# Gate matmuls begun one half tile later and packed six to a body, the gelu of a tile applied one half tile later

## The chip, the cores and the metric

The kernel runs on one core of a Trainium2 chip. The metric is the time of one launch on the device in microseconds (us), as the median of several runs. The engines named below are TensorE (PE in the profile; PEld is its weight load), VectorE (DVE), ScalarE (ACT), GpSimd (POOL) and SyncE (SP). A name with a q behind it (ACTq, DVEq, SPq) is the queue of that engine, that is the instructions that it issues or skips over without computing.

## The reference

Two layers, each a mixer (four kinds of attention over 256 tokens of width 2048) and a feed-forward block of 16384 experts, with a layer norm behind each. The change is in the feed-forward block, `peer_ffn`:

```python
q = x @ wq                                  # 8 heads, two halves of 128 each
s = einsum('blhpc,hpnc->blhpn', q, sub_keys)
s1, i1 = top_k(s[..., 0, :], 16)            # 16 of 128 first keys
s2, i2 = top_k(s[..., 1, :], 16)            # 16 of 128 second keys
cand = s1[..., :, None] + s2[..., None, :]  # 256 sums
top_s, pos = top_k(cand, 16); eidx = cidx[pos]
g = softmax(top_s)                          # gate of each chosen expert
h = einsum('td,tkd->tk', x, u[eidx])        # only the chosen experts
out = einsum('tk,tkd->td', g * gelu(h), v[eidx])
```

The kernel does not gather experts. It computes h for all 16384 experts, applies gelu to all, builds a dense table of gates (zero where an expert is not chosen) and multiplies.

## The kernel before, in words

**The stream.** The rows of u come as 128 tiles of 128x2048 (1 MB each) from the chip's memory, in order, through four buffers `raw0` to `raw3`. A tile is worked in two halves of 128x1024. For each half ACT rounds it to a high part (`split_hi`, L625, the copy at L634), DVE computes the low part as the difference (`split_lo`, L913, the subtraction at L917), and PE multiplies both with the tokens (`hidden`, L532: eight pairs of matmuls, L371 with 512 columns and L372 with 256). There are four buffers for the high parts and four for the low parts, so `split_hi` of half n+4 waits until `hidden` of half n is done, and ACT and DVE issue it in step n. Eight halves (four tiles) are called a body. A layer's u stream is 32 bodies, in four quarters of eight.

**A tile's result.** After the odd half of a tile, ACT copies one half of the result out of the bank (`take_cross`, L749, L754), DVE adds the other half (`add_cross`, L1221, L1223), ACT applies gelu in place (`gelu`, L756, L759) and issues a DMA that stores it in memory (L761). Tiles use banks 0 and 1 in turn, and `hidden` of a tile's even half waits for `add_cross` of the tile two before.

**The quarters.** For each of the two blocks of 128 tokens (b = 0, 1) there is a route quarter and a build quarter. In a route quarter DVE does, beside the splits, the top-k selection of one head per body (`route_body`, L1235). In a build quarter 32 gate steps are made, each for 4 tokens: POOL writes one-hot rows of the first keys (`first_keys`, L858: a copy at L861 and four operations at L864), DVE those of the second keys with their weights (`second_keys`, L1314: four operations at L1319), PE multiplies the two (`gate_step`, L542 ff., L551), and ACT copies the product into the table `gates` (`place_gates`, L765, L771). Each of these has two buffers: keys for step s wait until gate step s-2 is done.

**The first body of a build quarter** closes the softmax. DVE subtracts the largest score (`gate_weights`, L1301 and L1302) and then takes step 0. ACT applies Exp behind its step 1 (L797), which needs another function table than gelu, so a table load comes before it and another before the next gelu. DVE computes the sums and scales behind its step 2 (`gate_sums`, L1308 to L1310, semaphore `routed`). PE waits for `routed` behind `hidden` of half 3, turns the selected numbers with three transposes (L569), and ACT stores them (`sel_t`, L800) behind its own step 3. Then come gate steps behind halves 4 to 7. The other seven bodies have a gate step behind each odd half, the very last body behind halves 1, 3, 5 and 6.

**Order.** The order of each engine's work is written by hand. In step j of a body, ACT's `half_body` (L774) does `take_cross` if j is odd, `split_hi` of half j+4, and if j is odd `gelu` of the tile whose `take_cross` it has just done. DVE's `build_split` (L1338) does `add_cross` if j is odd and `split_lo` of half j+4. SP issues the loads of tiles in order, waits for the 32 gate steps of b = 0 before the loads of body 17, and writes the table of gates to memory between the loads of bodies 17 to 20. `place_gates` for b = 1 waits for these writes.

**Behind the stream** the same kind of loop runs over v (L590 to L592). It begins when the last `add_cross` is done. In its last step of the u stream DVE makes the first products of gelu and gate, and ACT their high part, `a_high` (L812), one step earlier in its order.

Of the kernel before, what the change touches and what calls it, by code (L numbers as in the profile page):

```python
# [15 lines left out]
P = 128  # L16
DEPTH, D, L = 2, 2048, 256
NB = L // P
# [6 lines left out]
NRAW, NSPLIT = 4, 4  # L25
BODY = 2 * NRAW
# [62 lines left out]
def build(nc, x_in, w_in, w_out, wq, keys, u_t, v_t, ln, sinks, lamp, subg, layer_consts,  # L89
# [6 lines left out]
    with ExitStack() as ctx:  # L96
# [47 lines left out]
        qk_t, at = region(0, 32, L)  # L144
        vals, at = region(at, NB, V_END)
# [9 lines left out]
        ln_gb, at = region(0, 2, D)  # L155
# [22 lines left out]
        STEPS = P // TG  # L178
        quarter = N_U // BODY // 4
        assert quarter == PH and STEPS == quarter * NRAW  # L180
        LAST_STEPS = (1, 3, 5, 6)
        PIECES = 16
        ROWS = NKEY // PIECES
        oh1 = [scr[:, i * 512:(i + 1) * 512].rearrange("p (t n) -> p t n", n=NKEY) for i in range(2)]
# [65 lines left out]
        with nc.Fori(0, DEPTH) as layer:  # L250
# [7 lines left out]
            with nc.Block() as block:  # L258
# [90 lines left out]
                def _(pe):  # L349
# [207 lines left out]
                    for b in range(NB):  # L557
                        if b == 0:
                            for j in range(BODY):
                                hidden(0, j, first=j < 4)  # L560
                        with pe.Fori(2 * b * quarter + (b == 0), (2 * b + 1) * quarter) as i:
                            for j in range(BODY):
                                hidden(i, j)
                        for j in range(BODY):
                            hidden((2 * b + 1) * quarter, j)
                            if j == 3:
                                pe.wait_ge(routed, b + 1)
                                for k in range(3):
                                    last = pe.transpose(bank[2][:, k * P:(k + 1) * P], sel[:, k, b, :], ident[:])  # L569
                                last.then_inc(sel_turned, 1)  # L570
                            if j >= 4:
                                gate_step(b * STEPS + j - 4, j % 2, first=(b == 0 and j < 6))
                        with pe.Fori(1, quarter - b) as i:
                            for j in range(BODY):
                                hidden(i + (2 * b + 1) * quarter, j)
                                if j % 2:
                                    gate_step(i * 4 + (b * STEPS + j // 2), j // 2 % 2)
                    for j in range(BODY):
                        hidden(4 * quarter - 1, j)
                        if j in LAST_STEPS:  # L580
                            gate_step(2 * STEPS - 4 + j // 2, j // 2 % 2)


                    def products(b, j, slot, start=False, stop=False):
# [39 lines left out]
                def _(act):  # L624
# [149 lines left out]
                    def half_body(i, j, first=False, last=False):  # L774

                        if j % 2:
                            take_cross(i, j // 2, i * 2 + j // 2 // 2, first=first and j < 4)
                        ahead = j + NSPLIT
                        if not last or ahead < BODY:
                            split_hi(AT_U, i + ahead // BODY, ahead % BODY)  # L780
                        else:
                            split_hi(AT_V, 0, ahead % BODY)
                        if j % 2:
                            gelu(i, j // 2)

                    for b in range(NB):
                        if b == 0:
                            for j in range(BODY):
                                half_body(0, j, first=True)
                        with act.Fori(2 * b * quarter + (b == 0), (2 * b + 1) * quarter) as i:  # L790
                            for j in range(BODY):
                                half_body(i, j)
                        for j in range(BODY):
                            half_body((2 * b + 1) * quarter, j)
                            if j == 1:
                                act.wait_ge(gate_arg, b + 1)
                                act.activation(sel[:, 2, b, :], sel[:, 2, b, :], ACT.Exp).then_inc(gate_exp, 1)  # L797
                            if j == 3:
                                act.wait_ge(sel_turned, b + 1)
                                act.activation(sel_t[:, :, b * P:(b + 1) * P], bank[2][:, 0:3 * P].rearrange("p (s t) -> p s t", s=3),  # L800
                                               ACT.Copy).then_inc(sel_stored, 1)
                            if j >= 4:
                                place_gates(b * STEPS + j - 4, (j - 4) * TG, j % 2, b)
                        with act.Fori(1, quarter - (b == 1)) as i:
                            for j in range(BODY):
                                half_body(i + (2 * b + 1) * quarter, j)
                                if j % 2:
                                    place_gates(i * 4 + (b * STEPS + j // 2), i * (4 * TG) + j // 2 * TG, j // 2 % 2, b)

                    def a_high(i, m):  # L810
                        act.wait_ge(prod_done, i * NRAW + (m + 1))
# [1 line left out]

                    for j in range(BODY):
                        half_body(4 * quarter - 1, j, last=True)
                        if j in LAST_STEPS:
                            place_gates(2 * STEPS - 4 + j // 2, P - 4 * TG + j // 2 * TG, j // 2 % 2, 1)
                        if j == BODY - 2:

                            a_high(0, 0)  # L820
# [80 lines left out]
                def _(dve):  # L901
# [432 lines left out]
                    def a_low(i, m):  # L1334
                        dve.wait_ge(ah_done, i * NRAW + (m + 1))
                        dve.tensor_tensor(al[m % 2], prod[m % 2], ah[m % 2].bitcast(F32), ALU.subtract).then_inc(al_done, 1)
# [7 lines left out]
                        else:  # L1344
                            split_lo(AT_U, i + (2 * b + 1) * quarter + ahead // BODY, ahead % BODY)

                    def build_body(i, b, last=False):

                        for j in range(BODY):
                            if b == NB - 1 and last and j == BODY - 1:  # L1350
                                dve.wait_ge(gate_evac, NB * STEPS)
                                product(0, 0, first=True)
                                product(0, 1, first=True)
                                a_low(0, 0)
                            build_split(i, b, j, last=last)
                            if j % 2 and not (last and j == BODY - 1):
                                second_keys(i * NRAW + (b * STEPS + j // 2 + 1), (j // 2 + 1) % 2)

                    def first_build_body(b):

                        gate_weights(b)
                        for j in range(BODY):
                            build_split(0, b, j)
                            if j == 2:
                                gate_sums(b)
                            if j == 3:
                                dve.wait_ge(sel_stored, b + 1)
                            if j >= 3:
                                second_keys(b * STEPS + j - 3, (j - 3) % 2, first=(b == 0 and j < 5))

                    for b in range(NB):
                        with dve.Fori(0, PH) as h:
                            route_body(h + 2 * b * quarter, b, h)
                        first_build_body(b)
                        with dve.Fori(1, quarter - 1) as i:
                            build_body(i, b)
                        build_body(quarter - 1, b, last=True)

                    def second_body(i, last=False):
                        for j in range(BODY):  # L1380
# [104 lines left out]
```

## Time and profile before

| | |
|---|---|
| median of 3 runs | 4180.57 us (4180.12 to 4183.09) |
| the profiled execution's own time | 4183.27 us |
| its span, first to last instruction | 4181.4 us |
| PE busy | 4052.1 us (97%), weight loads 3416.7 us (82%) |
| DVE busy | 2695.9 us (64%) |
| ACT busy | 1976.2 us (47%) |
| POOL busy | 515.8 us (12%) |
| mean granted TensorE clock | 0.959 of 2.4 GHz |

Busy time is an average over the whole span. What a stage is bound by is read from single stretches: from the time line of one engine, where an idle time stands in square brackets at the end of a row with what ended it, and from tables over stretches of time.

### The profile page before, as it was taken

To read this page: it belongs to the slowest core of one execution; us is meant where nothing else is said; L and a number is where in the kernel's file an instruction comes from. 1 tells how busy PE (TensorE), PEld (TensorE's weight loads), DVE (VectorE), ACT (ScalarE), POOL (GpSimd) and SP (SyncE) were. 2 spreads that over 40 slices of the span, in tenths; PEclk is the share of its full clock that TensorE was granted. 3 is DMA by queue.
4 is the path that set the end of the run, shared out by engine and by line. 5 is a ranking of instruction groups with operands and counts; after the bars stand their busy time and mean duration, and the time that the engine had idled before them with its cause. 6 is when DMAs were issued, how large, how long until landed. Compare 5 with 4: busy or idle time off the path is not lost. (4 is left out here: it accounts for less than half of the span.)

```text
span 4181.4 us, 64897 instructions
## 1 busy us (share of the span) xinstructions
PE 4052.1 (97%) x20356; PEld 3416.7 (82%) x20356; DVE 2695.9 (64%) x5308; ACT 1976.2 (47%) x2824; POOL 515.8 (12%) x728
## 2 busy tenths in 40 slices
PE   8999899999999999999899998999999999999997
PEld 7877788888888888888678777888888888888886
DVE  5656658767866555555656655686678665555556
ACT  4444344555455444444344443445554554444443
POOL 0100000351045000000001000003510550000000
PEclk9967999999999999999999779999999999999999
DMA  6512455557655666666545124555586556666664
GB/s 221 191 61 82 180 179 203 191 182 246 230 181 189 221 231 249 226 228 231 175 171 190 51 101 177 180 206 185 181 259 224 178 192 222 227 250 231 230 226 177
DMA packets 243054, 810.75 MB, mean 194 GB/s; under 512 B 24321, under 2 KB 157441, under 8 KB 157441
## 3 DMA queue, kind: packets, MB, share of 16 engines
q1 hardware_dynamic: 206080, 775.78, 52.9%
q10 hardware_dynamic: 36864, 33.57, 2.3%
q8 instruction: 62, 1.02, 0.1%
q14 instruction: 48, 0.39, 0.0%
HBM read 756.82 MB, written 52.43 MB: 194 GB/s over the span
## 5 line engine op out<-in xcount | busy, mean ns | idle before, releaser
L917 DVE TENSOR_TENSOR lo<-raw,hi 128x1024 fp32r<-128x1024 f32 x1312 | 1640.7, 1252 | 1194.4 <-ACT hi L634 1165.5
L634 ACT ACTIVATE hi<-raw 128x1024 fp32r<-128x1024 f32 x1312 | 1388.4, 1059 | 1366.9 <-PE bank L592 759.1
L371 PE MATMUL bank<-xhl,hi 128*128 128x512 f32 x4608 | 1641.4, 400 | 5.4 <-DVE xhl L923 2.8
L372 PE MATMUL bank<-xhl,lo 128*128 128x256 f32 x4608 | 1291.8, 280 | 0.0
L371 PEld LDWEIGHTS bank<-xhl,hi 128*128 128x128 f32 x4608 | 869.2, 189 | 212.0 <-DVE gelu_out L1223 3.9
L372 PEld LDWEIGHTS bank<-xhl,lo 128*128 128x128 f32 x4608 | 873.4, 190 | 0.0
L590 PE MATMUL bank<-hi,xhl 128*128 128x512 f32 x2048 | 797.1, 389 | 2.2 <-DVE gelu_out L1223 1.9
L592 PE MATMUL bank<-hi,xhl 128*128 128x512 f32 x2048 | 796.7, 389 | 0.0
L591 PE MATMUL bank<-lo,xhl 128*128 128x512 f32 x2048 | 796.7, 389 | 0.0
L590 PEld LDWEIGHTS bank<-hi,xhl 128*128 128x128 f32 x2048 | 384.4, 188 | 83.3 <-DVE gelu_out L1223 2.5
L592 PEld LDWEIGHTS bank<-hi,xhl 128*128 128x128 f32 x2048 | 384.4, 188 | 80.0
L591 PEld LDWEIGHTS bank<-lo,xhl 128*128 128x128 f32 x2048 | 384.4, 188 | 79.7
L864 POOL TENSOR_SCALAR scr<-iota_k,small 128x128 f32<-128x128 f32 x512 | 404.8, 807 | 12.2
L383 PE MATMUL bank<-hi,xhl 128*128 128x512 f32 (+1 forms) x896 | 352.6, 393 | 9.7 <-DVE lo L917 6.0
L385 PE MATMUL bank<-hi,xhl 128*128 128x512 f32 (+1 forms) x896 | 348.9, 389 | 0.0
L384 PE MATMUL bank<-lo,xhl 128*128 128x512 f32 (+1 forms) x896 | 348.6, 389 | 0.0
L874 POOL TENSOR_TENSOR x<-x,arena 128x512 f32<-128x512 f32 x8 | 13.4, 1679 | 1939.9 <-ACT x L731 1939.9
L754 ACT ACTIVATE gelu_out<-bank 128x256 f32<-128x256 f32 x256 | 97.0, 379 | 262.3 <-PE bank L372 262.3
L759 ACT ACTIVATE gelu_out<-gelu_out 128x256 f32<-128x256 f32 x256 | 105.9, 414 | 238.1 <-DVE gelu_out L1223 238.0
L383 PEld LDWEIGHTS bank<-hi,xhl 128*128 128x128 f32 x896 | 168.9, 189 | 43.5 <-issue 6.4
L385 PEld LDWEIGHTS bank<-hi,xhl 128*128 128x128 f32 x896 | 168.8, 188 | 34.8
L384 PEld LDWEIGHTS bank<-lo,xhl 128*128 128x128 f32 x896 | 169.2, 189 | 33.0
(131 smaller groups left out, 2692.7 us busy)
## 6 DMA issues: line engine op xcount, KB each, us to landing
raw<-u_t SPq DMA_DIRECT2D x256, 1024.0 KB, 4.8
raw<-v_t SPq DMA_DIRECT2D x256, 1024.0 KB, 4.8
raw<-w_in SPq DMA_DIRECT2D x84, 1024.0 KB, 4.8
raw<-w_out SPq DMA_DIRECT2D x32, 1024.0 KB, 4.8
raw<-wq SPq DMA_DIRECT2D x32, 1024.0 KB, 4.8
gelu_scratch<-gelu_out ACTq DMA_DIRECT2D x256, 128.0 KB, 1.7
scr<-gelu_scratch SPq DMA_DIRECT2D x256, 128.0 KB, 4.6
gates_scratch<-arena SPq DMA_DIRECT2D x32, 512.0 KB, 9.5
```

Of the source, the lines that this page charges most:

```text
L371: pe.matmul(acc[:], wh, xhl[:, c, :, :].rearrange("p a t -> p (a t)"), start=(c == 0), stop=False)
L372: return pe.matmul(acc[:, L:2 * L], wl, xh[:, c, :], start=False, stop=(c == DC - 1))
L383: pe.matmul(banks[b][:, 0:width], st_h, mh, start=(c == first_c), stop=False)
L384: pe.matmul(banks[b][:, 0:width], st_h, ml, start=False, stop=False)
L385: last = pe.matmul(banks[b][:, 0:width], st_l, mh, start=False, stop=(c == last_c))
L590: pe.matmul(y, a_h, vh, start=start, stop=False)
L591: pe.matmul(y, a_h, vl, start=False, stop=False)
L592: last = pe.matmul(y, a_l, vh, start=False, stop=stop)
L634: act.activation(hi[j % NSPLIT][:], half, ACT.Copy).then_inc(hi_done, 1)
L759: act.activation(gelu_out[m % 2][:], gelu_out[m % 2][:], ACT.Gelu).then_inc(gelu_done, 1)
L864: last = pool.tensor_scalar(oh1[p][:, t, :], iota_k[:], key_cols[p][:, t:t + 1], None, ALU.is_equal)
L917: dve.tensor_tensor(lo[j % NSPLIT][:], half, hi[j % NSPLIT][:].bitcast(F32), ALU.subtract).then_inc(lo_done, 1)
```

## The change

`hidden`, `gate_step`, `place_gates`, `first_keys`, `second_keys` and `gelu` stay as they are. Their places in the order change. In the first build body PE's wait for `routed` and the transposes stand behind half 4 instead of half 3, gate steps follow halves 6 and 7 only, ACT's copy of `sel_t` stands behind its step 4, and DVE's wait for it behind its step 4. The next five bodies have six gate steps each, behind halves 0, 1, 3, 4, 6 and 7. The last two bodies of each build quarter have none. `gelu` of a tile is applied in ACT's next even step, behind `split_hi`. The last tile's gelu stays in the last step.

```diff
-        LAST_STEPS = (1, 3, 5, 6)
+        STEP_OF = {0: 0, 1: 1, 3: 2, 4: 3, 6: 4, 7: 5}
+        PER_BODY = len(STEP_OF)
+        BUILD = (STEPS - 2) // PER_BODY
...
                         for j in range(BODY):
                             hidden((2 * b + 1) * quarter, j)
-                            if j == 3:
+                            if j == 4:
                                 pe.wait_ge(routed, b + 1)
...
-                            if j >= 4:
-                                gate_step(b * STEPS + j - 4, j % 2, first=(b == 0 and j < 6))
-                        with pe.Fori(1, quarter - b) as i:
+                            if j >= 6:
+                                gate_step(b * STEPS + j - 6, j % 2, first=(b == 0))
+                        with pe.Fori(1, 1 + BUILD) as i:
                             for j in range(BODY):
                                 hidden(i + (2 * b + 1) * quarter, j)
-                                if j % 2:
-                                    gate_step(i * 4 + (b * STEPS + j // 2), j // 2 % 2)
...
+                                if j in STEP_OF:
+                                    gate_step(i * PER_BODY + (b * STEPS + 2 - PER_BODY + STEP_OF[j]), STEP_OF[j] % 2)
+                        with pe.Fori(1 + BUILD, quarter) as i:
+                            for j in range(BODY):
+                                hidden(i + (2 * b + 1) * quarter, j)
...
-                        if j % 2:
+                        if j % 2 == 0 and not (first and j == 0):
+                            gelu(i, j // 2 - 1)
+                        if last and j == BODY - 1:
                             gelu(i, j // 2)
...
-                            if j == 3:
+                            if j == 4:
                                 act.wait_ge(sel_turned, b + 1)
...
+                    STEP_AHEAD = {1: -2, 2: -1, 4: 0, 5: 1, 6: 2, 7: 3}
...
+                            if j in steps:
+                                second_keys(i * PER_BODY + (b * STEPS + STEP_AHEAD[j]), STEP_AHEAD[j] % 2)
...
-                            if j == 3:
+                            if j == 4:
                                 dve.wait_ge(sel_stored, b + 1)
-                            if j >= 3:
-                                second_keys(b * STEPS + j - 3, (j - 3) % 2, first=(b == 0 and j < 5))
+                            if j >= 4:
+                                second_keys(b * STEPS + j - 4, j % 2, first=(b == 0 and j < 6))
```

## Rows read from the trace of the kernel before

**Rows 1.** PEld's time line, first build bodies (start us, us, engine, line, operation, [idle])
```profile
776.33 0.19 PEld L372 LDWEIGHTS bank<-xhl,lo 128*128 128x128 f32 x1
780.66 0.31 PEld L569 LDWEIGHTS bank<-ident,sel 128*128 128x128 f32 x3 [4.14 <-DVE sel L1310]
780.94 0.19 PEld L371 LDWEIGHTS bank<-xhl,hi 128*128 128x128 f32 x1
785.38 0.97 PEld L551 LDWEIGHTS bank<-scr 128*128 128x128 f32 x8
...
1171.03 0.19 PEld L372 LDWEIGHTS bank<-xhl,lo 128*128 128x128 f32 x1
1180.82 1.13 PEld L551 LDWEIGHTS bank<-scr 128*128 128x128 f32 x8
...
2857.59 0.19 PEld L372 LDWEIGHTS bank<-xhl,lo 128*128 128x128 f32 x1
2867.80 0.98 PEld L551 LDWEIGHTS bank<-scr 128*128 128x128 f32 x8
...
3252.94 0.19 PEld L372 LDWEIGHTS bank<-xhl,lo 128*128 128x128 f32 x1
3263.36 0.98 PEld L551 LDWEIGHTS bank<-scr 128*128 128x128 f32 x8
```

**Rows 2.** Waits of PEld over the span (us in total, times, longest)
```profile
PEld bank L569 <- DVE sel L1310: 17.6, 4, 4.8
```

**Rows 3.** PE in a stretch (us, busy, instructions, granted clock, DMA share, GB/s)
```profile
2865.00:2867.00 2.00, 2.00 (x8) 0.50 0.80 242
```

**Rows 4.** ACT's time line, first build body, layer 1, b = 0
```profile
2857.12 0.42 ACT L759 ACTIVATE gelu_out<-gelu_out 128x256 f32<-128x256 f32 x1 [1.53 <-DVE gelu_out L1223]
2857.95 1.28 ACT L797 ACT_TABLE_LOAD   x1 [0.41 <-ACT gelu_out L759]
2859.24 0.31 ACT L797 ACTIVATE sel<-sel 128x128 f32<-128x128 f32 x1
2859.46 1.04 ACT L634 ACTIVATE hi<-raw 128x1024 fp32r<-128x1024 f32 x1
```

**Rows 5.** DVE's time line, same body
```profile
2855.32 0.29 DVE L1302 TENSOR_TENSOR sel<-sel,small 128x128 f32<-128x128 f32 x1
2860.53 1.23 DVE L917 TENSOR_TENSOR lo<-raw,hi 128x1024 fp32r<-128x1024 f32 x1 [2.32 <-ACT hi L634]
2862.22 0.29 DVE L1310 TENSOR_TENSOR sel<-sel,small 128x128 f32<-128x128 f32 x1
```

**Rows 6.** Time lines of ACT and DVE, steps 5 and 6 of a route body
```profile
2754.66 0.42 ACT L759 ACTIVATE gelu_out<-gelu_out 128x256 f32<-128x256 f32 x1 [2.35 <-DVE gelu_out L1223]
2756.79 1.22 DVE L917 TENSOR_TENSOR lo<-raw,hi 128x1024 fp32r<-128x1024 f32 x1 [0.53 <-ACT hi L634]
```

**Rows 7.** PEld's time line, the same wait in two following route bodies
```profile
2789.36 0.19 PEld L371 LDWEIGHTS bank<-xhl,hi 128*128 128x128 f32 x1 [0.52 <-DVE gelu_out L1223]
...
2812.35 0.19 PEld L371 LDWEIGHTS bank<-xhl,hi 128*128 128x128 f32 x1 [0.60 <-DVE gelu_out L1223]
```

**Rows 8.** First matmuls L371 alone in route stretches, layers 0 and 1
```profile
670.00:770.00 100.00, 100.00 (x285) 1.00 0.59 209
...
2670.00:2770.00 100.00, 100.00 (x290) 1.00 0.56 194
```

**Rows 9.** PEld's time line, start of layer 1's route quarters, and a gate step
```profile
2666.49 0.19 PEld L371 LDWEIGHTS bank<-xhl,hi 128*128 128x128 f32 x1 [0.88 <-ACT scr L745]
...
3060.91 0.97 PEld L551 LDWEIGHTS bank<-scr 128*128 128x128 f32 x8
3061.81 0.19 PEld L371 LDWEIGHTS bank<-xhl,hi 128*128 128x128 f32 x1
```

**Rows 10.** PEld's time line, start of the v stream, layer 1
```profile
3458.66 0.19 PEld L590 LDWEIGHTS bank<-hi,xhl 128*128 128x128 f32 x1 [1.25 <-DVE gelu_out L1223]
```

**Rows 11.** All of line L864 (count, duration ns min/median/max, first and last start)
```profile
L864 POOL TENSOR_SCALAR scr<-iota_k,small x512: 594/602/1692, 783.0 to 3447.6; 128x128 f32<-128x128 f32 x171
```

More of the change, by code:

```diff
@@ L180, in build @@
         assert quarter == PH and STEPS == quarter * NRAW
-        LAST_STEPS = (1, 3, 5, 6)
+        STEP_OF = {0: 0, 1: 1, 3: 2, 4: 3, 6: 4, 7: 5}
+        PER_BODY = len(STEP_OF)
+        BUILD = (STEPS - 2) // PER_BODY
+        assert 2 + BUILD * PER_BODY == STEPS and BUILD < quarter - 1
         PIECES = 16
@@ L570, in _ @@
                                 last.then_inc(sel_turned, 1)
-                            if j >= 4:
-                                gate_step(b * STEPS + j - 4, j % 2, first=(b == 0 and j < 6))
-                        with pe.Fori(1, quarter - b) as i:
+                            if j >= 6:
+                                gate_step(b * STEPS + j - 6, j % 2, first=(b == 0))
+                        with pe.Fori(1, 1 + BUILD) as i:
                             for j in range(BODY):
                                 hidden(i + (2 * b + 1) * quarter, j)
-                                if j % 2:
-                                    gate_step(i * 4 + (b * STEPS + j // 2), j // 2 % 2)
[L578 to L581, printed above, removed]
+                                if j in STEP_OF:
[3 more added lines that the diff above has]
+                                hidden(i + (2 * b + 1) * quarter, j)
                     def products(b, j, slot, start=False, stop=False):
@@ L801, in _ @@
                                                ACT.Copy).then_inc(sel_stored, 1)
-                            if j >= 4:
-                                place_gates(b * STEPS + j - 4, (j - 4) * TG, j % 2, b)
-                        with act.Fori(1, quarter - (b == 1)) as i:
+                            if j >= 6:
+                                place_gates(b * STEPS + j - 6, (j - 6) * TG, j % 2, b)
+                        with act.Fori(1, 1 + BUILD) as i:
                             for j in range(BODY):
                                 half_body(i + (2 * b + 1) * quarter, j)
-                                if j % 2:
-                                    place_gates(i * 4 + (b * STEPS + j // 2), i * (4 * TG) + j // 2 * TG, j // 2 % 2, b)
+                                if j in STEP_OF:
+                                    at = 2 - PER_BODY + STEP_OF[j]
+                                    place_gates(i * PER_BODY + (b * STEPS + at), i * (PER_BODY * TG) + at * TG, STEP_OF[j] % 2, b)
+                        with act.Fori(1 + BUILD, quarter - (b == 1)) as i:
+                            for j in range(BODY):
+                                half_body(i + (2 * b + 1) * quarter, j)
                     def a_high(i, m):
@@ L815, in _ @@
                         half_body(4 * quarter - 1, j, last=True)
-                        if j in LAST_STEPS:
-                            place_gates(2 * STEPS - 4 + j // 2, P - 4 * TG + j // 2 * TG, j // 2 % 2, 1)
                         if j == BODY - 2:
@@ L1345, in build_split, with build_body @@
                             split_lo(AT_U, i + (2 * b + 1) * quarter + ahead // BODY, ahead % BODY)
-                    def build_body(i, b, last=False):
+                    STEP_AHEAD = {1: -2, 2: -1, 4: 0, 5: 1, 6: 2, 7: 3}
+                    def build_body(i, b, steps=STEP_AHEAD):
                         for j in range(BODY):
[L1350 to L1357, printed above, removed]
+                            build_split(i, b, j)
+                            if j in steps:
+                                second_keys(i * PER_BODY + (b * STEPS + STEP_AHEAD[j]), STEP_AHEAD[j] % 2)
                     def first_build_body(b):
@@ L1365, in first_build_body, with last_build_body @@
                                 gate_sums(b)
-                            if j == 3:
+                            if j == 4:
                                 dve.wait_ge(sel_stored, b + 1)
-                            if j >= 3:
-                                second_keys(b * STEPS + j - 3, (j - 3) % 2, first=(b == 0 and j < 5))
+                            if j >= 4:
+                                second_keys(b * STEPS + j - 4, j % 2, first=(b == 0 and j < 6))
+                    def last_build_body():
+                        for j in range(BODY):
+                            if j == BODY - 1:
+                                dve.wait_ge(gate_evac, NB * STEPS)
+                                product(0, 0, first=True)
+                                product(0, 1, first=True)
+                                a_low(0, 0)
+                            build_split(quarter - 1, NB - 1, j, last=True)
                     for b in range(NB):
@@ L1374, in _ @@
                         first_build_body(b)
-                        with dve.Fori(1, quarter - 1) as i:
+                        with dve.Fori(1, BUILD) as i:
                             build_body(i, b)
-                        build_body(quarter - 1, b, last=True)
+                        build_body(BUILD, b, steps=(1, 2, 4, 5))
+                        with dve.Fori(1 + BUILD, quarter - (b == 1)) as i:
+                            build_body(i, b, steps=())
+                    last_build_body()
                     def second_body(i, last=False):
```

## The prediction

> **What bounds the kernel now.** I read the page's busy shares first, then the chain of waits, then PE's weight loads in order of time through the u stream, since a matmul's own end is modelled and the start of its weight load is not. PE issues without a break nearly everywhere, so the question is where it does not. The reader is to see three places.
>
> First, in each of the four first build bodies PE stops behind half 3 until DVE's L1310, 17.6 us over four waits [rows 2]. Behind the stop the clock is at the lower of its two levels, 1.2 GHz, where it had been at 2.4 GHz without a break before it [rows 3], so half 4 is slow as well.
>
> Second, in layer 1's route quarters PE waits once or twice a body for DVE's `add_cross`; the same wait returns after 2812.35 - 2789.36 = 22.99 us [rows 7].
>
> Third, before the v stream it waits 1.25 us [rows 10].
>
> Two units follow. In layer 1 a pair of matmuls takes 100/290 = 0.345 us, in layer 0 100/285 = 0.351 us [rows 8]. Some records may be missing, and from pair to pair the loads step by 0.3467 and 0.3533 us. A half of eight pairs is thus 2.77 or 2.83 us, a body 22.2 or 22.6 us, at the same full clock and from the same code. A gate step takes 3061.81 - 3060.91 = 0.90 us [rows 9].
>
> **Step 1, the wait for `routed`.** From the last load of half 3 to gate step 0 the four bodies take 9.05, 9.79, 10.21 and 10.42 us [rows 1], 39.47 us in all. Without wait and slow clock it would be the last pair's rest of 0.23, the transposes 780.94 - 780.66 = 0.28 and a half of 2.77, so 3.28 us each. The excess is 39.47 - 13.12 = 26.3 us: 17.6 us of waits [rows 2], the rest the slow clock.
>
> Does all of it go? Count from the end of half 3, E = 2857.8 in layer 1, b = 0 (last load plus 0.23). Now: gelu at 2857.12, the DMA issue behind it, table load at 2857.95, Exp at 2859.24, the high part at 2859.46 [rows 4], DVE's low part at 2860.53 and L1310 done at 2862.51, E + 4.7 [rows 5]. DVE had its operand for Exp ready at 2855.61, E - 2.2, and Exp stood in ACT's queue behind a gelu that waited for DVE.
>
> New: no gelu stands between `split_hi` of step 1 and Exp. The copy and the high part of step 1 need half 1, done at E - 5.5, and end by E - 4.1. Table load and Exp run from E - 2.2 to E - 0.6, the high part to E + 0.4, the low part to E + 1.7, `gate_sums` takes from the end of the low part, 2861.76, to 2862.51, another 0.75 [rows 5]: `routed` at E + 2.4. PE asks for it at E + 2.8, behind half 4. In layer 0 the pace is slower and DVE further ahead, which gives more room. So the wait goes and with it the fall of the clock: -26.3 us. The margin is 0.4 us, and step 2 adds to it. Bounds: if only the half tile of 2.77 us helped, -11.1 us; with nothing left over, -26.3.
>
> The Trainium skill says in ScalarE: Activation LUTs, What ACT_TABLE_LOAD costs, that a switch of table takes about 2.66 us, 1.28 of load and 1.38 of drain. By that, `routed` could come as late as E + 3.8 and PE would still wait 1.0 us four times, leaving 4 us. This trace shows the load (1.28 us) with Exp 0.01 us behind it and only 0.41 us before it, DMA issue included [rows 4].
>
> **Step 2, gelu one half tile later.** In a route body ACT's gelu of step 5 starts at 2754.66 when DVE has added, its DMA and `split_hi` of step 6 queue behind it, and DVE idles 0.53 us for that high part [rows 6]. DVE is otherwise without a gap and is what holds PE there; its body is 22.99 us [rows 7] against PE's 22.2. With gelu behind `split_hi`, that high part is made when half 6 is done, some 4 us before DVE wants it. DVE's body becomes 22.99 - 0.53 = 22.46 us.
>
> DVE starts a route quarter with a lead. It lost 0.8 us a body against the fast pace, and the first stalls of PE come near 2777, after 4.8 bodies: the lead is 3.8 us. Eight bodies of 22.46 cost 8 x 0.27 = 2.2 us of it, so PE never waits. Layer 1's two quarters take from 2666.49 and from 3061.81 to 2857.82 and 3253.17, 191.3 us each [rows 1, 9]; 68 halves of 2.77 are 188.6. Gain 2.7 each, -5.5 us. In layer 0 DVE loses only 0.4 us a body against the slow pace and PE never waits for it: nothing to gain. The cover is the two tiles between a gelu and the reuse of its buffer; the store of 128 KB lands in 1.7 us by the page, far inside it. Bounds: 0 and -5.5.
>
> At the last step the high part of the first product now stands before `take_cross` with no gate step on PE to cover it: low part done 2.3 us behind half 6, product 0.5, high part 0.4, so `take_cross` begins at 3.3 us instead of the 2.8 at which half 7 ends. PE's wait of 1.25 us [rows 10] grows by about 0.6 us, in two layers +1.2 us (bounds 0 and +2).
>
> **Step 3, the packing.** PE's count of halves and gate steps stays the same. Behind a gate come either one half or two, so gates start 3.67 or 6.4 us apart. ACT does at most a high part, a gelu with its issue and one placing (1.06 + 0.9 + 1.1 = 3.1 us) in 3.67. POOL takes 4 x 0.602 [rows 11] + 0.3 = 2.7 us a step alone. DVE's key operations for a gate stand two halves before it. I find no wait in the bodies of six: 0.
>
> In the first body gate steps 0 to 3 come 3.67 us apart, as before, when they came 3.9 apart because POOL or DVE was just late. The copy of `sel_t` now ends 2.6 us behind half 4 (high part and gelu go first), the first keys of POOL 2.8 us later, and PE arrives at 6.0. I take the small waits as they are: 0, bounds +2 and -2.4.
>
> The two bodies without gates run at a body's 22.2 or 22.6 us. Behind a gate the pace was the fast one in two tiles of three before; a slow pace costs 0.43 a body, eight bodies: +0.9, bounds 0 and +3.4. SP's wait for the 32 gates ends earlier, its writes move ahead by a few halves, with loads that no one waits for: 0.
>
> **Sum.** -26.3 - 5.5 + 1.2 + 0.9 = -29.7 us. The profiled execution took 4183.3 and would take 4153.6; it was 2.7 us above the median of the runs, 4180.57, from which the same difference gives 4151 us.
>
> **Rivals.** (a) The pace of PE falls the other way. It is picked anew behind each stop and I can't derive it. If layer 1's route quarters run at 2.83 us a half, 2 x 68 x 0.053 = 7.2 us are lost and with all bodies without gates slow another 2.5: 4161 us. For it: layer 0 is slow in both quarters. Against: layer 1 is not. If layer 0 turns fast instead it is 4144; I count that with the forecast.
>
> (b) The wait is only shortened, since the margin of 0.4 us is thin and a chain of ten instructions sets it. PE then waits one to two us, which does not lower the clock (the 1.25 us before the v stream didn't, its loads go on at 0.23 us): 4 x 1.5 = 6 us more, with half the clock's gain at risk: 4157 to 4166, say 4161.
>
> (c) Slower than before: POOL. The longest L864 is 1692 ns against 602 [rows 11], one low part of DVE (1.2 us) longer. Gates behind halves 6, 7, 0 and 1 are the tight place: POOL may begin the third's keys when the first is done, and both third and fourth must be ready 10.1 us later, so it decides when a key step averages over 5.07 us. With one low part caught it is 3.8, with two 4.9, with three 6.0. At 6.0 PE waits 2 x 0.93 = 1.9 us in each of the 20 packed bodies, 37 us in all, which outweighs the gain: 4188. Against it: a body has eight low parts for six steps, and before the change a step caught one. The Trainium skill, SBUF — State Buffer, on its shared port pair, makes this an exclusive lock between these two engines, held for a whole instruction; by the maximum above the trace agrees.
>
> (d) The stop does not go but moves: PE passes `routed` and stops before gate step 0, where keys begin only after `sel_t`. The cover is 6.0 us against 5.4 needed. To eat the whole gain it must be over 5 us and drop the clock again: 4178.
>
> **How the numbers follow.** Forecast 0.68, (a) 0.14, (b) 0.09, (c) 0.05, (d) 0.04. A measurement of this kernel tells 0.2% (8.4 us) from no change. Forecast, (a) and (b) are faster by more than that: 0.91, of which I take 0.01 off for their tails; same 0.05, slower 0.05. Low end: 29.7 + 7.2 (layer 0 fast) + 2.4 (small waits gone) gives 4141. High end: (a) and (b) at 4161 with the 3 us by which runs differ, 4164.
>
> **What would show it.** Right: in all four first build bodies the load of L569 follows the last L372 by about 0.23 us with no idle time, the granted clock stays 1.00 through them, and last load of half 4 to gate step 0 is 6.1 us. In the route quarters DVE's 0.53 us at the sixth step and PE's waits for L1223 are gone. L864 may show more long operations but PE none waiting at L551 in packed bodies. The idle time before the first L590 is near 1.9 us. Wrong: an idle time over 1 us before L569 or L551, a clock of 0.5 anywhere in the u stream, or waits of PE that repeat with a body's period.

## The result, and the profile after the change

The kernel after the change takes 4158.15 us (median of 4 runs, 4155.05 to 4160.42) against 4180.92 for the kernel before (4 runs, 4180.12 to 4183.09). The ratio is 0.9944, its 95% interval 0.9930 to 0.9959: 22.8 us less, where 29.7 were forecast. In a later batch the same kernel took 4156.31 us (5 runs, 4151.98 to 4158.62), a ratio of 0.9940, 0.9927 to 0.9954. The profiled execution took 4160.42 us, with a span of 4158.6 and a mean granted clock of 0.962 (before 0.959).

The page's first part, busy us with shares and instruction counts, and its fourth, the chain that ended last:

```profile
PE 4043.6 (97%) x20356; PEld 3411.6 (82%) x20356; DVE 2689.6 (65%) x5308; ACT 1969.0 (47%) x2824; POOL 516.6 (12%) x728
...
PE 48%; DVE 1%; ACT 0%; issue 0%; POOL 0%; DVEq 0%; ACTq 0%; POOLq 0%
```

The engines do the same work as before, PE 8.5 us less of it. PE's weight-load rows from behind half 3 of the first build body to gate step 0, layer 1, b = 0 (line numbers are up by 2 to 4 for PE and ACT, by 6 for DVE and POOL), answer to [rows 1]:

```profile
2847.14 0.19 PEld L375 LDWEIGHTS bank<-xhl,lo 128*128 128x128 f32 x1
2847.37 0.19 PEld L374 LDWEIGHTS bank<-xhl,hi 128*128 128x128 f32 x1
...
2849.96 0.19 PEld L375 LDWEIGHTS bank<-xhl,lo 128*128 128x128 f32 x1
2850.20 0.37 PEld L572 LDWEIGHTS bank<-ident,sel 128*128 128x128 f32 x3
2850.53 0.19 PEld L374 LDWEIGHTS bank<-xhl,hi 128*128 128x128 f32 x1
...
2856.78 0.97 PEld L554 LDWEIGHTS bank<-scr 128*128 128x128 f32 x8 [0.64 <-POOL scr L870]
```

Half 3 ends at E = 2847.4. The transposes (L572) follow half 4 after 2850.20 - 2849.96 = 0.24 us with no idle time: the stop of [rows 2] is gone. In each of the four bodies a small one is left, in three before gate step 0 and in the last before gate step 1. PE's granted clock over the same stretch (us, busy, instructions, clock, DMA share, GB/s), where [rows 3] had 0.50 behind the stop:

```profile
2850.00:2870.00 20.00, 19.68 (x125) 1.00 0.52 178
```

PEld's waits over the span (us in total, times, longest), which answer to [rows 2, 7, 10]:

```profile
PEld bank L592 <- DVE gelu_out L1229: 3.3, 2, 1.7
PEld bank L554 <- POOL scr L870: 2.3, 4, 0.6
```

The wait for `routed` and the repeated waits for `add_cross` are not among them. The wait before the v stream has grown from 1.25 us [rows 10] to 1.66 us in layer 0 and to 1.61 in layer 1:

```profile
3435.86 0.19 PEld L592 LDWEIGHTS bank<-hi,xhl 128*128 128x128 f32 x1 [1.61 <-DVE gelu_out L1229]
```

ACT's and DVE's rows of the same first build body answer to [rows 4, 5]:

```profile
2842.32 1.05 ACT L636 ACTIVATE hi<-raw 128x1024 fp32r<-128x1024 f32 x1
2843.39 1.28 ACT L801 ACT_TABLE_LOAD   x1
2844.68 0.31 ACT L801 ACTIVATE sel<-sel 128x128 f32<-128x128 f32 x1
2844.91 1.06 ACT L636 ACTIVATE hi<-raw 128x1024 fp32r<-128x1024 f32 x1
...
2852.36 0.49 ACT L804 ACTIVATE sel_t<-bank 128x384 f32<-128x384 f32 x1 [0.41 <-ACT gelu_out L761]
```

```profile
2841.19 0.29 DVE L1308 TENSOR_TENSOR sel<-sel,small 128x128 f32<-128x128 f32 x1
...
2846.01 1.22 DVE L923 TENSOR_TENSOR lo<-raw,hi 128x1024 fp32r<-128x1024 f32 x1 [1.38 <-ACT hi L636]
...
2847.70 0.29 DVE L1316 TENSOR_TENSOR sel<-sel,small 128x128 f32<-128x128 f32 x1
```

`routed` is set at 2847.99, E + 0.6. Last, the count of first matmuls L374 in the windows of [rows 8], layers 0 and 1:

```profile
670.00:770.00 100.00, 100.00 (x284) 1.00 0.61 208
...
2670.00:2770.00 100.00, 100.00 (x284) 1.00 0.63 207
```

Layer 1 had 290 and now has 284, at the same granted clock of 1.00 and with PE never idle. There lies most of what is missing from the gain.

### The profile page after: what moved, and what is told of

Read it like the earlier page. It is cut to its first block and busy times, and to the rows that moved or that the text cites. A ratio compares the mean times of both kernels' runs of the same rounds, so it can differ in the third digit from the quotient of the medians.

```text
span 4158.6 us, 64863 instructions
## 1 busy us (share of the span) xinstructions
PE 4043.6 (97%) x20356; PEld 3411.6 (82%) x20356; DVE 2689.6 (65%) x5308; ACT 1969.0 (47%) x2824; POOL 516.6 (12%) x728
## 3 DMA queue, kind: packets, MB, share of 16 engines
q8 instruction: 64, 1.05, 0.1%
## 5 line engine op out<-in xcount | busy, mean ns | idle before, releaser
L374 PE MATMUL bank<-xhl,hi 128*128 128x512 f32 x4608 | 1638.5, 400 | 4.2 <-DVE xhl L929 2.8
L374 PEld LDWEIGHTS bank<-xhl,hi 128*128 128x128 f32 x4608 | 865.8, 188 | 210.8 <-DVE xhl L929 3.6
L870 POOL TENSOR_SCALAR scr<-iota_k,small 128x128 f32<-128x128 f32 x512 | 405.6, 807 | 12.3
L1229 DVE TENSOR_TENSOR gelu_out<-bank,gelu_out 128x256 f32<-128x256 f32 x256 | 108.5, 424 | 119.3 <-ACT gelu_out L756 103.5
```

What stands on the lines that cost most here:

```text
L374: pe.matmul(acc[:], wh, xhl[:, c, :, :].rearrange("p a t -> p (a t)"), start=(c == 0), stop=False)
L870: last = pool.tensor_scalar(oh1[p][:, t, :], iota_k[:], key_cols[p][:, t:t + 1], None, ALU.is_equal)
L1229: dve.tensor_tensor(gelu_out[m % 2][:], bank[m % 2][:, 0:L], gelu_out[m % 2][:], ALU.add).then_inc(summed, 1)
```

## The experiments

All kernels ran beside the kernel before, on three chips; before took 4180.89 us in the first batch (15 runs) and 4180.5 in the second (9). Besides the profile's rows I use the mean distance of pairs over a stretch without gates: from the load of its first L374 to that of its last, divided by the steps from pair to pair. As long as PE has no wait in it, it is either 346.7 ns (fast) or 353.3 ns (slow); a stretch with waits is a mixture, as shown below. After the change the stretches are 2655.17 to 2849.84 (551 steps), 2999.60 to 3239.51 (679 steps, the last two bodies of one build quarter and the next route quarter) and 3389.07 to 3433.94 (127 steps), and the same in layer 0. None has a wait. Five of the six are slow; only layer 0's last is fast.

### The gelu alone

The kernel before, with nothing moved but `gelu`:

```diff
-                        if j % 2:
+                        if j % 2 == 0 and not (first and j == 0):
+                            gelu(i, j // 2 - 1)
+                        if last and j == BODY - 1:
                             gelu(i, j // 2)
```

> The kernel before with step 2 alone: gelu in the next even step, gate steps and the wait for routed where they were. If the order in ScalarE's queue carries the gain (my reading of the trace of after, where routed is done 0.6 us behind half 3), PE waits 0.5 to 2.4 us before the transposes in the four first build bodies, the clock stays at its upper level, and the time is 4158 to 4165 us. If the half tile carries it, PE still waits 4 us, the clock falls, and the time is 4175 to 4181.

Measured: 4166.17 us (10 runs), ratio 0.9967, 0.9957 to 0.9977. PE's stop in the first build body, layer 1, b = 0:

```profile
2853.35 0.31 PEld L569 LDWEIGHTS bank<-ident,sel 128*128 128x128 f32 x3 [0.73 <-DVE sel L1312]
...
2859.65 0.97 PEld L551 LDWEIGHTS bank<-scr 128*128 128x128 f32 x8 [3.25 <-POOL scr L866]
```

The wait for `routed` falls from 17.6 to 5.0 us over four bodies by this part alone, and the clock stays at 1.00. But gate step 0 still stands behind half 4, and PE stops there for POOL (8.9 us over the four), which the expectation had not counted: the time is just over its 4158 to 4165. No PE wait for `add_cross` repeats in layer 1's second route quarter, and that stretch runs fast for most of its length.

### The packing alone

The kernel after, with `gelu` back in the odd step:

```diff
-                        if j % 2 == 0 and not (first and j == 0):
-                            gelu(i, j // 2 - 1)
-                        if last and j == BODY - 1:
+                        if j % 2:
                             gelu(i, j // 2)
```

> The changed kernel with gelu back in the odd step: steps 1 and 3 without step 2. By the chain of rows before (routed at E + 4.0 to E + 4.7) PE still waits 1.2 to 1.9 us behind half 4 in each first build body, too short for the clock to fall: 6 us over the changed kernel, 4164 us, and up to 4 more if the route quarters run at the fast pace and wait for VectorE again. If the half tile alone carried the gain, the time is that of the changed kernel, 4158.

Measured: 4167.29 us (6 runs), ratio 0.9968, 0.9955 to 0.9980.

```profile
2851.08 0.31 PEld L572 LDWEIGHTS bank<-ident,sel 128*128 128x128 f32 x3 [1.32 <-DVE sel L1314]
...
2858.03 0.97 PEld L554 LDWEIGHTS bank<-scr 128*128 128x128 f32 x8 [1.06 <-POOL scr L868]
```

Waits: 6.4 us for `routed`, 4.5 for POOL, again with the clock at 1.00, and 3.3 us before the v stream: that growth belongs to the packing already, so my reason for it (the gelu's move) was wrong in part. Each part alone gives about 14 us and both 23, since either of them shortens the same stop and gets the clock back. The last of the wait for `routed` goes only with both. This kernel holds both the half tile and the packing; no run takes these two apart.

### Idle matmuls: can the pace be changed?

Four small matmuls, and in a second kernel one, are added before each of the six stretches. They write a bank that is overwritten before it is read; the output is untouched.

```diff
+                    def nudge():
+                        for _ in range(4):
+                            pe.matmul(bank[3][:, 0:P], ident[:], ident[:], start=True, stop=True)
+
...
+                    nudge()
...
+                        nudge()
```

> The changed kernel with four more matmuls of the kind of a gate step (identity by identity, into bank 3, used by nobody) ahead of each stretch without gates: 0.9 us each, six of them. Theory P: the pace of a stretch (2.77 or 2.83 us a half) is a state that each gate step advances by one of three, one of which is slow; the stretches that were slow (all but the last of layer 0) turn fast behind one more step: 84 halves of 0.053 less in two places and 16 in one, about 10 us less, 4.5 paid, 4152 to 4154 us, and the stretch that starts a layer may turn too. Rival R: the pace is drawn by chance or by other engines: no stretch turns in a regular way, and the time is 4158 + 5.

> As the kernel with four more matmuls, but with one (two passes of TensorE) in each of the six places, 0.2 us each. Theory P with a count of passes modulo three (a gate step is eight passes, 8 mod 3 = 2; one matmul is 2 passes, the same rest): the same stretches turn fast, for a quarter of the price, 4149 to 4152 us. If the state goes by time or by whole gate steps, no such turn or another one: 4155 to 4161.

Measured: with four 4157.41 us (4 runs, ratio 0.9945, 0.9929 to 0.9962), with one 4158.35 (4 runs, 0.9947, 0.9931 to 0.9964); both within the spread of the kernel after. Theory P of the first expectation, a fixed count in which all slow stretches turn, is refuted: with four, three of the five turned and the fast one became slow. With one, its count of passes fails too. But stretches did change. First matmuls L374 with four, layers 0 and 1, the stretch behind the keys:

```profile
670.00:770.00 100.00, 100.00 (x290) 1.00 0.60 211
...
2670.00:2770.00 100.00, 100.00 (x290) 1.00 0.62 212
```

And with one, where the stretch behind the keys stays slow:

```profile
2670.00:2770.00 100.00, 100.00 (x284) 1.00 0.62 210
```

The last stretches came out fast in both layers with one and slow in both with four. In layer 1's last one (40 us of it), with one and then in the kernel after, slow:

```profile
3390.00:3430.00 40.00, 40.00 (x117) 1.00 0.65 224
```

```profile
3390.00:3430.00 40.00, 40.00 (x114) 1.00 0.63 220
```

That can't be put down to the idle matmul: in a second execution of the kernel after (below) both last stretches were fast without one. Only the stretch behind the keys shows an effect, in both layers.

How long does a pace last? The kernel with the gelu alone has a stretch with a single wait (layer 0's second route quarter):

```profile
1132.79 0.19 PEld L371 LDWEIGHTS bank<-xhl,hi 128*128 128x128 f32 x1
1133.29 0.19 PEld L371 LDWEIGHTS bank<-xhl,hi 128*128 128x128 f32 x1 [0.20 <-DVE gelu_out L1225]
...
1166.84 0.19 PEld L371 LDWEIGHTS bank<-xhl,hi 128*128 128x128 f32 x1
```

From its start at 977.83 to 1132.79 the 447 steps took 346.7 ns each, from 1133.29 to 1166.84 the 95 steps took 353. So the pace is a state that lasts while PE has no wait. A wait of 0.2 us can turn it, and in the stretch behind the keys four small matmuls ahead of it do. It is worth 1.9% of the pairs that it holds for. With four, layer 1's long second stretch began fast too (as it did in that second execution without them), and in it PE does catch up with DVE again:

```profile
3175.40 0.19 PEld L374 LDWEIGHTS bank<-xhl,hi 128*128 128x128 f32 x1 [0.37 <-DVE gelu_out L1235]
...
3198.12 0.19 PEld L374 LDWEIGHTS bank<-xhl,hi 128*128 128x128 f32 x1 [0.29 <-DVE gelu_out L1235]
```

DVE's rows at the same place, one body apart:

```profile
3175.26 1.22 DVE L929 TENSOR_TENSOR lo<-raw,hi 128x1024 fp32r<-128x1024 f32 x1
...
3197.99 1.22 DVE L929 TENSOR_TENSOR lo<-raw,hi 128x1024 fp32r<-128x1024 f32 x1
```

DVE's body is 22.73 us, where 22.46 were predicted and 22.99 measured before [rows 7]. The step gave 0.26 us a body, half of what I took it for.

### The two small waits, and the pace behind the keys

The next kernel stores `sel_t` before ACT's step 4 instead of behind it, and lets DVE make the first two products of v one step earlier:

```diff
                         for j in range(BODY):
+                            if j == 4:
+                                act.wait_ge(sel_turned, b + 1)
...
                             half_body((2 * b + 1) * quarter, j)
...
-                            if j == 4:
-                                act.wait_ge(sel_turned, b + 1)
...
-                            if j == BODY - 1:
+                            if j == BODY - 2:
                                 dve.wait_ge(gate_evac, NB * STEPS)
                                 product(0, 0, first=True)
                                 product(0, 1, first=True)
+                            if j == BODY - 1:
                                 a_low(0, 0)
```

> The changed kernel with two orders mended: in the first build body ScalarE stores sel_t ahead of its step 4 instead of behind it, and VectorE makes the first two products of the v stream one step earlier. If the waits that are left at gate step 0 (0.64, 0.62, 0.64, 0.46 us) come from the late sel_t, they go, and the wait before the v stream falls from 1.6 to 1.25 us: 3.1 us less, 4155 us, if the pace of TensorE's stretches stays. If GpSimd is late for another reason (held by VectorE), the waits stay and the time is 4158.

Measured: 4151.26 us (5 runs, 4149.34 to 4152.40), ratio 0.9929, 0.9915 to 0.9942. PEld's waits:

```profile
PEld bank L592 <- DVE gelu_out L1229: 2.5, 2, 1.3
PEld bank L374 <- DVE gelu_out L1229: 2.1, 10, 0.2
```

The gate wait is gone, the wait before the v stream is back at 1.25 us. Together that is some 3 us of the 5.0 by which it lies below the kernel after of the same batch. The other 2 are pace, by the two profiled executions: layer 0's second stretch began fast here and took 1163.83 - 925.87 = 237.96 us against 239.90. The ten waits of at most 0.25 us for `add_cross` stand in that stretch and its like in layer 1. They turn the pace back and forth: of the 679 steps in layer 0's, 445 are fast, 227 slow and 7 have a wait.

With four idle matmuls besides, in one place only, ahead of each layer's u stream:

```diff
+                    for _ in range(4):
+                        pe.matmul(bank[3][:, 0:P], ident[:], ident[:], start=True, stop=True)
```

> The same two orders and four idle matmuls (0.9 us) only ahead of each layer's u stream. With the four more matmuls in all six places both of these stretches ran at the fast pace (346.7 ns a pair), in ten of the twelve stretches seen so far without them (or with one) they ran slow. If these matmuls set the pace, 68 halves of 0.053 us less in each layer for 0.9: 5.4 us under the kernel with the two orders alone, 4150 us. If the pace is drawn at each stop without regard to them, 1.8 us more than that kernel, 4157, and the two stretches slow in most runs.

Measured: 4146.05 us (5 runs, 4145.41 to 4148.51), ratio 0.9918, 0.9904 to 0.9931. It is 5.2 us below the same kernel without them, and the fastest of all. The added work is four small matmuls in each layer; the stretch behind it takes 2839.40 - 2648.10 = 191.3 us for 551 steps. The first 511 take 346.7 ns each; the last 39, behind one step that is 0.03 us longer, take 353.

The unaltered kernel after ran in the same batch:

> The changed kernel once more, unaltered, for the pace of its stretches in a second execution. If the pace follows from the program alone, all stretches without gates run at the same pace as in the first trace (slow but for the last one of layer 0). If it is drawn anew at stops, at least one of the six differs, and the times spread over the 5 us that runs of it showed. The time is 4155 to 4160 us.

4156.31 us, as told above. Its stretch behind the keys was slow in both layers again; of the others, layer 1's second (up to its first wait) and third came out fast in this profiled execution and not in the first. So for these two a run decides. For the one behind the keys none was seen to: without idle matmuls that stretch was slow in 15 of the 16 seen in all kernels (the "ten of the twelve" of the expectation above, which takes in the kernel with one, is nine of ten in the traces kept), the one exception being layer 1 of the kernel before, on which the forecast rested.

Is it that enough idle matmuls must be there? The same kernel with two and with three:

> The kernel with the two orders mended and two idle matmuls instead of four ahead of each layer's u stream (0.45 us). One left the stretch slow, four made it fast. If any shift beyond the first does it, both stretches run at 347 ns a pair and the time is 4145 us. If four are needed because their number matters, the stretches run at 353 ns and the time is 4151.

> The same with three idle matmuls (0.67 us). By the same two readings: both stretches fast and 4146 us, or slow and 4151 us. With the runs of zero, one, two and four it shows whether the effect has a threshold or alternates.

One run each, 4147.06 us with two and 4150.15 with three. First matmuls L374, with two, then with three:

```profile
2670.00:2770.00 100.00, 100.00 (x289) 1.00 0.62 213
```

```profile
2670.00:2770.00 100.00, 100.00 (x284) 1.00 0.64 213
```

One and three leave the stretch slow, two and four make it fast, in both layers each time; with none it is slow but for that one exception. It is not a threshold, then. The number matters in a way that looks like even and odd, from five values, two of them run once. Each idle matmul also starts the stretch about 0.2 us later; no run tells the number from this shift, or shows what in the chip remembers it.

### How near is POOL?

POOL makes one and then two more key operations in each key step, into a tile that no one reads:

```diff
+        extra = sb("extra", [P, 2, NKEY])
...
+                        for t in range(1):
+                            pool.tensor_scalar(extra[:, p * 1 + t, :], iota_k[:], key_cols[p][:, t:t + 1], None, ALU.is_equal)
```

> The changed kernel with one more GpSimd operation in each key step (the same comparison, written to a tile that nobody reads): five instead of four. In packed bodies a key step takes 3.6 us in the trace of the changed kernel, so 4.4 to 4.5 with it. A packed body of 27.6 us has room for six steps of 4.6 us. If rival (c) is right about its mechanism and this bound is the one that counts, TensorE waits only in the first build bodies, 0.6 us more in each of the first gates: 4158 to 4166 us. If key steps already set the pace of packed bodies, 20 bodies grow by 6 x 0.8 us each: 4250 us.

> The changed kernel with two more GpSimd operations in each key step: six instead of four. A key step takes 3.6 us in packed bodies of the changed kernel, so 4.9 to 5.3 with them, over the 4.6 us that six steps have in a body of 27.6 us. If GpSimd's sum per body is the bound, each packed body grows to 29.4 to 31.8 us, 20 bodies, 36 to 84 us: 4195 to 4245 us. By the bound that my prediction gave (5.07 us for two steps in a row), the growth would be 0 to 10 us: 4160 to 4180.

One run each. With one more: 4166.5 us, at the upper end of what was expected, and all waits of gate steps stand before the first four of each build quarter (two groups of waits, eight each):

```profile
PEld bank L555 <- POOL scr L873: 6.3, 8, 1.6
PEld bank L555 <- issue: 3.2, 8, 0.6
```

With two more: 4192.6 us, 13 over the kernel before in the same batch (4179.53). Now the packed bodies stop as well (PE's time line, two gate steps of one body):

```profile
2912.66 1.15 PE L555 MATMUL bank<-scr 128*128 128x128 f32 x8
2917.20 1.15 PE L555 MATMUL bank<-scr 128*128 128x128 f32 x8 [0.60 <-POOL scr L873]
```

These two gate steps, behind halves 0 and 1, lie 2917.20 - 2912.66 = 4.54 us apart instead of 3.7. The waits stand there alone, about 0.45 and 0.9 us in each packed body behind the first one, and a body came out at 2941.58 - 2912.65 = 28.93 us instead of 2891.80 - 2864.15 = 27.65 (gate step behind half 0, from body to body). POOL itself has no pause left:

```profile
2880.00:3020.00 140.00, 137.22 (x205) 1.00 0.46 160
```

A key step thus takes 28.93 / 6 = 4.8 us. By parts: POOL's 117 operations of L873 in this window took 92.56 us, 0.79 each, and the 59 added ones 41.40 us, 0.70 each, so 4 x 0.79 + 2 x 0.70 + 0.3 = 4.9. What counts is six steps in a body, 27.65 / 6 = 4.6 us, not my 5.07 for the tightest two of them; the place where PE then waits is the one that rival (c) named. Neither of the two ranges expected (4195 to 4245 and 4160 to 4180) holds the time, which lies just under the first. In the kernel after, a step takes:

```profile
2874.00:2996.00 122.00, 84.58 (x104) 1.00 0.49 169
```

26 steps of four operations (L870 alone), 84.58 / 26 = 3.25 us, with the copy and the gaps about 3.6. One more operation is covered in the packed bodies, two are not.

## Why the prediction was right, and where it was not

**Step 1, the wait for `routed`, -26.3.** Right, and with more room than thought. No wait, no fall of the clock, four times. `routed` came at E + 0.6, not at E + 2.4, and PE asked for it 2.2 us later. DVE had the operand for Exp ready at 2841.48, E - 5.9 and not E - 2.2, so the table load began right behind the high part of step 1, at E - 4.0. In the slow pace of this stretch (below) DVE is further ahead of PE. The sentence on the Trainium skill (ScalarE: Activation LUTs, What ACT_TABLE_LOAD costs) had 2.66 us for a switch with 1.0 us of wait left over. The trace does not show its drain on either side: 1.28 us of load, Exp 0.01 us behind it, and the end of the high part 0.02 us before it (2842.32 + 1.05). With or without those 1.4 us PE would not have waited here. In the second execution of the kernel after, PE had caught up with DVE in layer 1's second route quarter, the tight case for which the forecast had its margin, and there too it had no stop before the transposes:

```profile
3234.56 0.29 DVE L1316 TENSOR_TENSOR sel<-sel,small 128x128 f32<-128x128 f32 x1
```

```profile
3236.01 0.36 PEld L572 LDWEIGHTS bank<-ident,sel 128*128 128x128 f32 x3
```

`routed` was set at 3234.85, 1.16 us before PE asked for it, where 0.4 were forecast.

**Step 2, the gelu, -5.5 + 1.2.** The mechanism holds, its worth does not, and here the missing microseconds are. Layer 1's route quarter took 192.2 us (2655.17 to 2847.4) where 188.6 were predicted and 191.3 were taken before. PE does not wait in it at all. It runs at the slow pace: 68 halves of 2.83 us. The second quarter did the same, so the term came out at 2 x 0.9 = +1.8 us instead of -5.5, 7.3 us worse: rival (a) to its 7.2. I had taken the fast pace for a property of layer 1, from one trace [rows 8]; behind the keys it was the one fast case in sixteen, and in the second quarter the two executions of this kernel differ. A second mis-sizing lay beneath. I took DVE's whole 0.53 us of [rows 6] as gained, though 0.13 of it is the usual gap between two of its operations and 0.12 us came back at step 4. DVE then loses 0.54 us a body to a fast PE (22.73 - 22.19), and the lead of 3.8 us is used up after 7 bodies. The second stretch has ten and a half, as it begins with the two bodies without gates: begun fast it took 237.96 us, only 1.9 less than slow, where 679 x 6.6 ns would be 4.5: the seven waits cost 1.1 us and the 227 slow steps between them 1.5. So a fast layer 1 would have given some 3 of the 5.5 us, not all. The wait before the v stream grew by 0.4 each, +0.8 instead of +1.2, and the packing alone shows the same growth.

**Step 3, the packing, 0 + 0.9.** Right for the bodies of six: gate steps 3.67 and 6.44 us apart, none waits. The two bodies without gates were slow in three of four quarters: +2.6. "The small waits as they are" holds in size (nine waits, 2.9 us in all, in the trace of before) and not in place: four of 0.46 to 0.64 us, 2.3 in all. Three stand before gate step 0, because POOL's first keys wait for a copy of `sel_t` that stands behind a gelu (2852.36). The fourth stands before gate step 1, whose four key operations took 4.32 us. The kernel with the two orders mended has none of the four. The store of gelu lands later than I wrote:

```profile
gelu_scratch<-gelu_out ACTq DMA_DIRECT2D x256, 128.0 KB, 3.9
```

It was 1.7 us in the page of before. The gelu's new place is what changed it in the main: the median is 3.2 us with the gelu alone and 1.7 with the packing alone. ACT now waits for it ten times, 24.8 us in all and 3.6 at most. None of that reaches PE, so "far inside" the two tiles was true for PE alone.

**Sum.** -26.3 + 1.8 + 0.8 + 2.6 = -21.1, against 4160.42 - 4183.27 = -22.9 measured between the profiled executions. The four quarters, from stream start to stream start, gained 5.1, 6.5, 5.7 and 5.8 us, 23.1. Of the 2 us between, 0.6 are the small waits at the gate steps (2.9 us before, 2.3 after). The rest is within the gate stretches, where the pace changes from half to half in both kernels, and I have not told it apart.

**Rivals.** (a) is what happened, on top of a right forecast for the rest: 4161 said, 4158 measured. (b) did not: the wait went whole; with either part alone it is what one gets (5.0 and 6.4 us left), and no such short stop lowered the clock. (c) did not happen, and its deciding point was set 0.5 us too high. The Trainium skill, SBUF — State Buffer, on the shared port pair, says that one engine holds it for a whole instruction, and the trace agrees: the longest of POOL's key operations (L870) is 1677 ns against a median of 598, 1.08 us more and so within one low part (1.22 us); a key step averages 3.25 us of operations instead of 2.4, one caught about every 1.4 steps. (d) happened in its harmless form, at most 0.64 us instead of five.

## What to carry to other kernels

Look at what one late wait costs behind itself: of 26.3 us, 17.6 were waits and the rest was the slow clock after them. Do not extend a rate seen in one stretch of one trace to a changed kernel; count it in every like stretch and every run first, and if it takes two values, carry both in the sum. A rate that changes at a wait is to be counted between waits. When an idle gap is taken as gain, subtract the gap that the engine leaves anyway.

## What the runs showed of the hardware

- A stream of pairs of float32 matmuls, 512 and 256 columns, ran at 346.7 or 353.3 ns a pair with the granted clock at 1.00 in both. It kept the one or the other as long as it had no wait (679 steps slow, 511 fast), and waits of 0.2 us turned it at times. Small matmuls ahead of the stretch behind the keys turned it (0, 1 and 3: slow, but for one case with 0; 2 and 4: fast), and eight of them in a kernel gave 5.2 us. Why stays open.
- PE stopped for 3.25 us, a half behind another stop of 0.73, and was granted 1.00 afterwards; after stops of 4.0 to 4.8 us it was granted 0.50 [rows 2, 3].
- A store of 128 KB that ACT's queue issues landed in 1.7 us (median) in the kernel before and with the packing alone, in 3.2 us with the gelu alone and in 3.9 in the kernel after, with the same bytes. It changed with the gelu's place, and so with the moment of issue; what the store then meets was not tried.
